# A two-block transformer kernel on one core: one barrier fewer at each stage end, a wait moved from ScalarE to SyncE, and other banks for the second token-major product

## The reference

```
p = _split_in(x @ w_in)                     # the projection: q, k, v, gates, indexer inputs ...
ya = _mixer_a(a_q, a_k, a_v, rpb_table)     # three dilated attention patterns with a distance bias
yb = _mixer_b(b_q, b_ckv, b_iq, ...)        # attention over the top 128 keys by an indexer score
yc = _mixer_c(...); yd = _mixer_d(...)      # two linear-attention mixers
merged = sum(gates * (ys @ w_branch)); x = layer_norm(ALPHA * x + merged @ w_out)
x = layer_norm(ALPHA * x + _moe(x, 32 experts, top 2))
for l in range(2):                          # second block
    x = hybrid_layer(x, mem, ...)           # reads rms_norm(mem) @ w_mem_kv, its own mixers, a feed-forward
```

## Time and profile before

| | |
|---|---|
| median of 3 runs | 2733.21 us (2732.72 to 2737.58) |
| the profiled execution | a span of 2737.7 us from the first to the last instruction; no other time of it is given, so the span stands for its own time (the slowest of the three runs took 2737.58) |
| mean granted clock of TensorE | 0.970 |
| TensorE busy | 2591.2 us, 95% |
| VectorE busy | 1083.1 us, 40% |
| ScalarE busy | 793.0 us, 29% |
| GpSimd busy | 953.7 us, 35% |
| DMA | 339.46 MB, mean 124 GB/s |

### The profile page before, as it was taken

How to read it: one execution, slowest core, us unless ns; L and a number is a source line. 1 busy time by engine, 2 the same in 40 slices (tenths; PEclk the granted TensorE clock), 3 DMA queues, 4 the chain that set the end, 5 groups by cost and what they waited for, 6 DMA issues and landing times. The chain is left out here.

```text
span 2737.7 us, 30875 instructions
## 1 busy us (share of the span) xinstructions
PE 2591.2 (95%) x12456; PEld 1936.9 (71%) x12456; DVE 1083.1 (40%) x1764; ACT 793.0 (29%) x1128; POOL 953.7 (35%) x313
## 2 busy tenths in 40 slices
PE   8878789999889999899999999999998999999998
PEld 6666578788433336675888888887765888888886
DVE  4765454445421113376444421122276444311111
ACT  3024321322211113426222332222327223322311
POOL 4564100244123332320444444444320444444443
PEclk9988899899989999999999999999999999999999
DMA  4421010232669995340322222222340222222223
GB/s 167 155 108 70 31 39 1 100 108 93 250 248 388 389 385 216 108 101 7 108 93 94 100 99 92 95 106 92 114 93 17 94 106 93 93 92 106 94 93 123
DMA packets 83021, 339.46 MB, mean 124 GB/s; under 512 B 34262, under 2 KB 34646, under 8 KB 47296
## 3 DMA queue, kind: packets, MB, share of 16 engines
q1 hardware_dynamic: 63640, 315.24, 31.7%
q10 hardware_dynamic: 5416, 13.82, 1.4%
q0 software_dynamic: 13824, 8.44, 1.0%
HBM read 379.99 MB, written 28.74 MB: 149 GB/s over the span
## 5 line engine op out<-in xcount | busy, mean ns | idle before, releaser
L167 POOL TENSOR_TENSOR w_lo<-w_raw,w_hi 128x2048 fp32r<-128x2048 f32 x150 | 698.8, 4658 | 1333.7 <-ACT w_hi L160 1314.8
L193 PE MATMUL bank<-xh,w_hi 128*128 128x512 f32 x1784 | 709.4, 398 | 35.3 <-DVE w_lo L399 11.1
L194 PE MATMUL bank<-xl,w_hi 128*128 128x512 f32 x1784 | 698.6, 392 | 0.0
L195 PE MATMUL bank<-xh,w_lo 128*128 128x512 f32 x1784 | 698.3, 391 | 0.0
L193 PEld LDWEIGHTS bank<-xh,w_hi 128*128 128x128 f32 x1784 | 337.7, 189 | 120.4 <-issue 31.3
L160 ACT ACTIVATE w_hi<-w_raw 128x2048 fp32r<-128x2048 f32 x152 | 290.4, 1911 | 378.3 <-PE bank L193 356.2
L194 PEld LDWEIGHTS bank<-xl,w_hi 128*128 128x128 f32 x1784 | 337.7, 189 | 74.0 <-issue 5.0
L195 PEld LDWEIGHTS bank<-xh,w_lo 128*128 128x128 f32 x1784 | 337.5, 189 | 70.8
L193 PE MATMUL bank<-ha,w_hi 128*128 128x512 f32 x480 | 186.7, 389 | 0.0
L194 PE MATMUL bank<-hb,w_hi 128*128 128x512 f32 x480 | 186.7, 389 | 0.0
L195 PE MATMUL bank<-ha,w_lo 128*128 128x512 f32 x480 | 186.7, 389 | 0.0
(11 more groups left out here) (588 smaller groups left out, 3758.3 us busy)
## 6 DMA issues: line engine op xcount, KB each, us to landing
w_raw<-weights SPq DMA_DIRECT2D x189, 1024.0 KB, 4.8
ring<-weights SPq DMA_DIRECT2D x49, 1024.0 KB, 9.9
before_halves<-weights SPq DMA_DIRECT2D x18, 1024.0 KB
res<-weights SPq DMA_DIRECT2D x16, 1024.0 KB
distance_bias<-distance_bias_once ACTq DMA_DIRECT2D x8, 512.0 KB
na_bias<-grid_bias SPq DMA_DIRECT2D x16, 240.0 KB, 6.7
strips<-distance_bias SPq DMA_DIRECT2D x8, 448.0 KB, 4.0
ring<-picked_rows SPq DMA_DIRECT2D x6, 512.0 KB, 6.4
```

The source lines that it names most:

```text
L167: engine.tensor_tensor(self.lo[:, s, :], self.raw[:, s, :], self.hi[:, s, :].bitcast(F32), ALU.subtract).then_inc(self.split, 1)
L193: self.released(pe.matmul(out, hi, moving[0], start=start, stop=False))
L194: pe.matmul(out, hi, moving[1], start=False, stop=False)
L195: return pe.matmul(out, lo, moving[0], start=False, stop=stop)
```

## The change

Three edits. The second barrier of each stage end is gone; so that the next stage doesn't meet semaphores that are still to be cleared, each stage's names get the suffix `_0` or `_1` by turns, and a stage's semaphores are given back only once the next stage has allocated its own. ScalarE's wait for the eight bias copies becomes a wait of SyncE, in `loads_end`, behind `k.gates.begin`. The second token-major product goes to banks 0 to 3, and waits for all 21 tile copies (`product_copied`) instead of the copy of the first product.

```diff
 def stage(k, *names, drained=False):
     nc = k.nc
-    with ExitStack() as ctx:
-        sems = [ctx.enter_context(nc.semaphore(n)) for n in names]
-        with nc.Block(no_gpsimd_drain=not drained) as block:
-            yield (block, *sems)
-        engines = (nc.sync, nc.scalar, nc.vector, nc.tensor, nc.gpsimd)
-        for n, s in enumerate(sems):
-            engines[n % len(engines)].sem_clear(s)
-        nc.all_engine_barrier()
+    held = ExitStack()
+    k.stages += 1
+    sems = [held.enter_context(nc.semaphore(f"{n}_{k.stages % 2}")) for n in names]
+    k.cleared_before.close()
+    k.cleared_before = held
+    with nc.Block(no_gpsimd_drain=not drained) as block:
+        yield (block, *sems)
+    engines = (nc.sync, nc.scalar, nc.vector, nc.tensor, nc.gpsimd)
+    for n, s in enumerate(sems):
+        engines[n % len(engines)].sem_clear(s)
...
             k.gates.begin(sp)
+            if "loads_end" in aside_run:
+                aside_run["loads_end"](sp, *aside_sems)
...
                 if m:
-                    pe.wait_ge(rows_copied, m)
+                    pe.wait_ge(product_copied, tiles)
...
-                    last = ws.product_tm(pe, [k.bank[4 + q][:, 0:width] for q in range(nt)], still, width // 128,
+                    last = ws.product_tm(pe, [k.bank[4 - 4 * m + q][:, 0:width] for q in range(nt)], still, width // 128,
...
-                    last = dve.tensor_copy(rows[:, q, :], k.bank[4 + q][:, 0:width])
+                    last = dve.tensor_copy(rows[:, q, :], k.bank[4 - 4 * m + q][:, 0:width])
...
             act.dma_start(bias_dram[h:h + 1, :, :], row).then_inc(bias_stored, 16)
-        act.wait_ge(bias_stored, 16 + 128)
+
+    def loads_end(sp, rows_in, bias_ready, bias_copied, bias_stored):
+        sp.wait_ge(bias_stored, 16 + 128)
```

More of the change, by code:

```diff
@@ L85, in __init__ @@
         self.nc, self.dram, self.tensors = nc, dram, 0
+        self.cleared_before, self.stages = ExitStack(), 0
 class Order:
@@ L1087, in vector @@
                 bias_copied, 1)
-    return names, dict(loads=loads, scalar=scalar, tensor=tensor, vector=vector)
+    return names, dict(loads=loads, loads_end=loads_end, scalar=scalar, tensor=tensor, vector=vector)
 def memory_rows(k, mem, scaled, gains, total):
@@ L3124, in build @@
         k = Kernel(nc, dram)
+        ctx.callback(lambda: k.cleared_before.close())
         k.bank = [ctx.enter_context(nc.psum_tensor(f"bank{b}", [128, 512], F32)) for b in range(8)]
```

## The result

The changed kernel takes 2715.67 us (median of 5 runs, 2713.43 to 2717.72), the kernel before beside it 2736.32 (5 runs, 2732.72 to 2737.58). The ratio is 0.9935, with a 95% interval of [0.9923, 0.9946]: 17.8 us less (14.8 to 21.1), where 27.2 were forecast. The time lies in the stated range of 2699 to 2716, at its upper end, and outside the 2702 to 2711 that the forecast itself allowed. One execution of the kernel before, beside the first four experiments, took 6263.65 us and enters no number here.

The account below looks back on a forecast made before the run. TensorE, busy 95% of the span, was taken as the bound, with time won at its stops and lower clock. Projection 18.0, barriers 8.3 and clock 0.9 sum to 27.2 us: 2733.2 to 2706.0, own range 2702 to 2711, stated 2699 to 2716.

Parts of the forecast that it names:

- The moved wait: Projection stage: ScalarE's square no longer waits for the bias copies; 8.2 us of TensorE stop plus 2.8 of lower clock, 11.0.
- SyncE's wait costs nothing: Projection stage: SyncE reaches the wait about 154 us, after the copies landed by 119.33, so cost 0.
- The second product in other banks: Projection's end: second product follows the first at once, saving 4.4 us of pause and 2.6 of lower clock, 7.0.
- Rival B: Projection: VectorE or GpSimd, running late, takes the second product's gain back; saves 19 us, 2714; chance 0.08.
- No second barrier: At the 21 stage ends: removing the second barrier saves 8.3 us in all, with ends 0 and 15.
- Rival A: Stage ends: barriers are hidden, each next stage waits later for something else; saves 18 to 20 us, 2714; chance 0.10.
- The clock at stage starts: Stage starts: shorter pauses may leave TensorE's higher clock granted; 0.9 us gained for all.
- rival D: Stages from 186 to 374 us: shifted pauses make the lower clock hold nearly throughout; slower, 2755 us; chance 0.01.

Follow-up runs that it names:

- the first four experiments: e1 to e4, kernels that each hold only some parts of the change, measured on one chip beside the kernel before at 2733.03 us.
- e3: Changed kernel with the second barrier put back and the second product in banks 4 to 7 again, so the moved wait alone: 2727.35 us, ratio 0.9976.
- e8: The kernel before, unchanged, run once more with its profile: 2734.40 us.
- e5: The kernel before, with four of the eight bias copies issued behind ScalarE's work on the memory rows: 2726.59 us, ratio 0.9975.
- e4: Changed kernel with the second barrier put back and the bias wait back on ScalarE, so the other banks alone: 2726.57 us, ratio 0.9970.
- e2: Changed kernel with the second barrier put back, so the moved wait and the other banks together: 2719.19 us, ratio 0.9956.
- e1: Changed kernel with the projection of the kernel before, so only the second barriers are gone: 2726.80 us, ratio 0.9979.
- e12: The changed kernel, unchanged, run again beside a kernel with added filler matmuls: 2712.98 us, ratio 0.9923 to the kernel before.
- e6: The changed kernel, unchanged, run again on another chip with profile: 2712.77 us, ratio 0.9917 to the kernel before.

## Why the prediction was right and wrong

**The moved wait: mechanism right, size too large.** The square starts at 102.39 (said: 102.5), VectorE is in time, and TensorE does not stop. The term was "Sum of this part 11.0 us". The step that failed is "TensorE would go on at 117.36 and not at 125.52: 8.2 us", with the 2.8 of low clock behind it: that is the price in one execution, and the copies' landing at 119.33 was the latest of all those seen. Against that very execution the term holds: 11.0 said, and e3's stage ends 11.65 us before it, at 171.08 against 182.73. Against e8, the same kernel, it is 6.9 (171.08 against 177.96), and the timings say 6.6 and 6.8 (e3, e5). That is 4.1 to 4.4 us of the missing ones. The prediction subtracted a sum of one execution from a median of others, and bounded every part but the landing time itself. It had noted that this execution was 4.5 us above the median (by span against span it is more, 6.3) and did not ask where these us lay.

**SyncE's wait costs nothing: right.** SyncE issues the next stage's loads at 165.50 like its neighbours, and no stage end waits for it.

**The second product in other banks: right.** 7.0 forecast. The timing of e4 gives 8.2 (4.9 to 11.2), and the stage ends give 171.08 - 164.85 = 6.2 (e3 to e2). The last matmul starts at 162.92 (said: 162.7), VectorE copies the first product at 154.58 (said: 153.9), GpSimd is done with the last chunk at 154.5 (said: 153.7). Rival B, whose stop would have been at these places, did not come.

**No second barrier: the pauses right, the time smaller.** 8.3 forecast, and the pauses are 8.6 shorter; behind the experts 1.04 (said: 1.0). But the timing of that part alone is 5.7 (3.3 to 8.2). Rival A is out, since the pauses did shrink. Of what is missing, 0.5 lie between span and device time; the rest is of the size of what the stages' insides gave back in the mean of the profiles, but e1 alone doesn't prove it.

**The clock at stage starts: wrong in sign.** The step reads "Shorter pauses may leave the higher clock granted ... I take 0.9 for all". In place of 0.9 gained, the low clock rose by some 10 us in the mean of six profiles each (3 to 10 by the clocks of all runs), and the insides of stages by 3.1. This is rival D's mechanism at less than a tenth of its size. It was given 0.01 because its price was worked out only for the extreme, and the argument "no pause becomes longer" was too weak: the changed kernel has shorter pauses at all 21 stage ends than before, and more low clock behind the projection. The same section of the Trainium skill that the prediction named ("TensorE: Matmul & The Clock Gate", on the clock gate) bears on this: the number of slow matmuls after a start differs from run to run of one kernel. By it the term was to be 0. The runs agree that it varies (e12 has 10.4 us less low clock than the first profile of the same kernel), but in the mean it was not zero here.

The sum with the measured terms: 6.9 + 6.2 + 8.5 - 0.5 - 3.1 = 18.0 us, against 17.8 (14.8 to 21.1) in the first comparison and 22.7 and 21.0 in the later ones; that it meets the first so closely is luck. Of the 9.2 us between 27.2 and 18.0, 4.9 are the projection's 18.0 against 13.1, 4.0 the clock (0.9 + 3.1), and 0.3 the barriers (8.3 against 8.0). So the steps that failed are two: the stop at the bias copies was priced by one execution with a late landing, and the clock was booked as a gain. The first is shown by e3, e5 and e8; the second is read from profiles and clocks, and its cause is open.

Open: why stage 5 keeps its longer length in all kernels without the barrier and in e2; why the low clock behind the projection is higher in the mean and not only moved. Twelve profiles of kernels that differ in other ways too do not settle it. The changed kernel's three comparisons (17.8, 22.7 and 21.0) differ by 5 us, which is the size of the terms in question.

## What to carry to other kernels

A stall that ends with a DMA's landing has the length that the landing had in that execution. Before it is booked, take a second execution, or keep half of it as the range. Each removed pause should be priced twice, as a pause and by what follows it: where a good part of the time is at the lower clock, single later stages differed by 1.0 to 2.8 us between kernels that do the same work in them. Where TensorE must pause at stage ends anyway, a few matmuls with unused results were worth 8 to 11 us here, at least as much as the removal of the barriers there (5.7).

## What the runs showed of the hardware

- The same eight 512 KB copies, issued at the same place in the program, had landed at 114.8 in one execution and at 119.3 in another of the same kernel, and TensorE's stop was 3.90 or 7.99 us for it.
- A clear of a semaphore takes 56 ns on TensorE's queue and TensorE's eight follow one another in about 0.13 us each (165.1 to 166.0); the other engines' are 30 to 54 ns.
- A stage of 112 matmuls with many short waits (stage 5) lasts 19.1 us at a granted clock of 0.72 and 22.0 at 0.66, with the same work of every other engine.
- Runs of one kernel on one chip are spread over 4 us (after, five runs) to 15 us (e6, six runs) of 2700.
- The device time is 1.8 us above the span in the kernels that end with a second barrier and 2.3 us in the changed kernel, so 0.5 us of a shorter span was not gained.
